# State-space stage of a two-block sequence model: decays from broadcast running sums, floor and exponential on ScalarE, mask on the scores, skip term in PSUM

## What is computed

```python
dt = softplus(dt_raw + dt_bias); a = -exp(a_log)
a_cs = cumsum(dt * a)                        # in each chunk of 128 tokens, one sum for each of 16 heads
cb = einsum("bclgn,bcsgn->bcgls", cc, bc)    # 2 groups of heads, state size 128
y_diag = einsum("bcgls,bcghls,bcsghp->bclghp", cb, exp_segsum(a_cs), xdt)   # exp(a_cs[l] - a_cs[s]) for s <= l, else 0
states = einsum("bclgn,bcghl,bclghp->bcghpn", bc, exp(a_cs[-1] - a_cs), xdt)
carry = carry * exp(a_cs[-1]) + states       # from chunk to chunk
y_off = einsum("bclgn,bcghpn,bcghl->bclghp", cc, prev, exp(a_cs))
y = y_diag + y_off + xs * d_skip
g = y * silu(z); ssm = g * rsqrt(mean(g * g) over a group + 1e-5) * w
```

## Time and profile before

| | before |
|---|---|
| median of three runs | 3471.3 us |
| profiled execution | 3469.94 us |
| its span | 3468.1 us |
| TensorE busy | 3187.7 us (92%) |
| VectorE busy | 1530.2 us (44%) |
| ScalarE busy | 1038.9 us (30%) |
| GpSimd busy | 1080.5 us (31%) |
| mean granted TensorE clock | 0.959 |

### The profile page before, as it was taken

The page is one execution under the profiler, slowest core; times in us unless marked ns, Lnnn a source line. Parts: engine busy times, 40 slices in busy tenths (PEclk is TensorE's granted clock), DMA queues, the critical chain, the costliest instruction groups (busy, mean ns, idle before and its releaser), DMA issues. The chain is left out here.

```text
span 3468.1 us, 49486 instructions
## 1 busy us (share of the span) xinstructions
PE 3187.7 (92%) x21000; PEld 2545.8 (73%) x21016; DVE 1530.2 (44%) x2122; ACT 1038.9 (30%) x1822; POOL 1080.5 (31%) x698
## 2 busy tenths in 40 slices
PE   5998799777999998989999998879899999988798
PEld 3885489665888877878777776658787777766587
DVE  3999645424222224341244343871312443438713
ACT  3012333313222222222244343530122444435401
POOL 2443022103333324323333332333233333323342
PEclk8999899898999999999999999989999999999899
DMA  5113200222111111222121224004221212240142
GB/s 198 49 49 118 102 4 4 77 87 74 48 48 48 48 30 61 97 79 75 49 79 49 67 92 154 11 34 143 84 76 48 80 49 68 91 157 8 36 144 76
DMA packets 210596, 250.71 MB, mean 72 GB/s; under 512 B 9280, under 2 KB 164032, under 8 KB 207968
## 3 DMA queue, kind: packets, MB, share of 16 engines
q1 hardware_dynamic: 199584, 208.02, 18.5%
q10 hardware_dynamic: 10240, 37.75, 2.8%
q0 software_dynamic: 576, 2.10, 0.2%
HBM read 199.60 MB, written 46.14 MB: 71 GB/s over the span
## 5 line engine op out<-in xcount | busy, mean ns | idle before, releaser
L1875 PE MATMUL PS<-x_high_sb,w_high_sb 128*128 128x512 f32 x1312 | 530.1, 404 | 0.0
L1875 PE MATMUL PS<-x_high_sb,w_low_sb 128*128 128x512 f32 x1312 | 518.2, 395 | 0.0
L1875 PE MATMUL PS<-x_low_sb,w_high_sb 128*128 128x512 f32 x1312 | 517.4, 394 | 0.0
L1875 PEld LDWEIGHTS PS<-x_high_sb,w_high_sb 128*128 128x128 f32 x1312 | 247.0, 188 | 76.1 <-issue 23.9
L1875 PEld LDWEIGHTS PS<-x_high_sb,w_low_sb 128*128 128x128 f32 x1312 | 246.9, 188 | 57.8
L360 PE MATMUL PS<-h_high_sb,up_high_sb 128*128 128x512 f32 x704 | 275.0, 391 | 13.5 <-POOL up_low_sb L1445 13.5
L1875 PEld LDWEIGHTS PS<-x_low_sb,w_high_sb 128*128 128x128 f32 x1312 | 247.3, 189 | 52.3
L360 PE MATMUL PS<-h_low_sb,up_high_sb 128*128 128x512 f32 x704 | 274.6, 390 | 0.0
L360 PE MATMUL PS<-h_high_sb,up_low_sb 128*128 128x512 f32 x704 | 274.6, 390 | 0.0
L1495 DVE SCALAR_TENSOR_TENSOR z_sb<-PS,cols_sb,z_sb 128x1023 f32<-128x1023 f32 x88 | 112.8, 1282 | 348.9 <-ACT z_sb L1476 342.5
L2112 DVE CUSTOM_DVE_ANT_0 scores_sb<-PS,alibi_sb,sinks_sb 128x256 f32<-128x256 f32 (+1 forms) x256 | 104.4, 464 | 341.8 <-PE PS L1893 341.6
(11 more groups left out here) (409 smaller groups left out, 6461.8 us busy)
## 6 DMA issues: line engine op xcount, KB each, us to landing
w_raw_sb<-w_in SPq DMA_DIRECT2D x102, 512.0 KB, 3.9
up_raw_sb<-w_up SPq DMA_DIRECT2D x44, 512.0 KB, 3.9
ada_slots_sb<-ada_w SPq DMA_DIRECT2D x16, 1024.0 KB, 5.5
w_raw_sb<-w_out SPq DMA_DIRECT2D x64, 256.0 KB, 2.8
xbc<-staged_sb ACTq DMA_DIRECT2D x24, 512.0 KB, 2.6
down_raw_sb<-w_down SPq DMA_DIRECT2D x44, 256.0 KB, 2.6
xbc_sb<-xbc SPq DMA_DIRECT2D x2, 5376.0 KB, 19.1
attn<-HT_sb ACTq DMA_DIRECT2D x8, 1024.0 KB, 4.9
```

The source lines that it names most:

```text
L1875: last = pe.matmul(PS[:, bank, :], a[:, n % 2, k], b[:, k, cols], start=k == 0 and a is WH and b is HH, stop=k == KT - 1 and a is WL)
```

## The change

`StepSizes` gains one TensorE transpose of the negated running sums, one ScalarE copy and one DMA that writes them to DRAM as 128 rows (chunk and head) of 128 tokens. In `state_space` the R products, the bf16 constants and the copy of X are gone. For each chunk one DMA loads the 16 rows of negated sums, each broadcast to all 128 partitions (1 MB), into one of three slots of E. ScalarE adds the positive sums as bias and floors the difference at zero (16 Relu instructions), and one Exp with scale -1 covers all 16 heads. The triangle mask is applied to the scores on VectorE (`masked`). The decays are multiplied in two instructions of eight heads (`weigh`). VectorE makes both products of x straight from PSUM (`inputs`), with dt folded into the decay to the end once. The skip term is a product with a diagonal matrix that TensorE adds up in the same PSUM banks as YD (`within`). The state has two buffers, and its scaling moves to GpSimd. The sums of squares are taken as 32-column products with 64 tokens each, so that root and reciprocal work on 64 columns, and four small products spread the result (`spread`). The order of each engine's program is new.

```diff
+        act.wait_ge(s.turned, 1)
+        nc.scalar.copy(self.tmp[:, 0], self.m.PS[:, 3, 0:TT * SH]).then_inc(s.ex, 1)
+        act.wait_ge(s.ex, 4)
+        act.dma_start(self.rows_d, self.tmp[:, 0]).then_inc(s.row_out, 16)
...
+        pe.transpose(self.m.PS[:, 3, 0:TT * SH], self.NA[:], self.m.const("ident")).then_inc(self.s.turned, 1)
...
-                    pe.wait_ge(step.s.ex, 3)
+                    pe.wait_ge(step.s.ex, 4)
...
+            act.wait_ge(step.s.row_out, 16)
...
+def state_space(m, d_skip, xbc_d, gate_d, rows_d, DT, A, NA, EI, DE, CD):
+    SLOTS = 3
-        RS = alloc(m, ctx, "inverse_rms", [P, 2, SG, P])
+        RS = alloc(m, ctx, "inverse_rms", [P, 2, HD])
-        E = alloc(m, ctx, "decays", [P, SH, P])
-        XS = alloc(m, ctx, "x_by_token", [P, DI])
-        XDT = alloc(m, ctx, "x_dt", [P, DI])
-        XDE = alloc(m, ctx, "x_dt_decayed", [P, DI])
+        E = alloc(m, ctx, "decays", [P, SLOTS, SH, P])
+        XDT = alloc(m, ctx, "x_dt", [P, 2, DI])
+        XDE = alloc(m, ctx, "x_dt_decayed", [P, 2, DI])
-        tmp = alloc(m, ctx, "y_tmp", [P, DI])
-        BC = alloc(m, ctx, "b_and_cb", [P, 512])
-        S = alloc(m, ctx, "state", [P, DI])
-        DS = alloc(m, ctx, "skip_rows", [P, SH])
+        BC = alloc(m, ctx, "b_and_cb", [P, 2, 512])
+        S = alloc(m, ctx, "state", [P, 2, DI])
+        SKIP = alloc(m, ctx, "skip_diagonal", [P, KT, P])
...
+            def rows(c):
+                sp.dma_start(E[:, c % SLOTS], rows_d[c * SH:(c + 1) * SH].unsqueeze(0).to_broadcast([P, SH, P])
+                             ).then_inc(row_in[c % SLOTS], 16)
+            rows(0)
+            sp.dma_start(XB[:, :, 0:P], xbc_d[:, :, 0:P].rearrange("k p t -> p k t")).then_inc(s.x_in0, 16)
+            sp.dma_start(skip[:], d_skip.to_broadcast([P, SH])).then_inc(s.skip_in, 16)
+            rows(1)
+            sp.dma_start(XB[:, :, P:T], xbc_d[:, :, P:T].rearrange("k p t -> p k t")).then_inc(s.x_in1, 16)
+            rows(2)
             sp.dma_start(ZS[:], gate_d.rearrange("k p t -> p k t")).then_inc(s.z_in, 16)
+            for c in range(SLOTS, TT):
+                sp.wait_ge(s.yd, c - SLOTS + 1)
+                rows(c)
...
+            def b_and_cb(c):
+                    pe.wait_ge(s.moved, c)
+                    pe.wait_ge(s.cb, c)
+                for g in range(SG):
+                    pe.transpose(PS[:, 4, g * P:(g + 1) * P], XB[:, KT + g, cols(c)], m.const("ident"))
+                for g in range(SG):
+                    last = pe.matmul(PS[:, 4, (2 + g) * P:(3 + g) * P], XB[:, KT + g, cols(c)],
+                                     XB[:, KT + SG + g, cols(c)], start=True, stop=True)
+                last.then_inc(s.b, 1)
+            def x_turned(c):
+                if c:
+                    pe.wait_ge(s.st_out, c)
...
+                last.then_inc(s.x, 1)
+            def from_state(c):
+                pe.wait_ge(s.st_out, c)
+                pe.wait_ge(s.y, c)
...
+                last.then_inc(s.yo, 1)
+            def to_state(c):
+                pe.wait_ge(s.moved, c + 1)
+                pe.wait_ge(s.xde, c + 1)
...
+                last.then_inc(s.st, 1)
+            def within(c):
+                pe.wait_ge(s.xdt, c + 1)
+                if c:
+                    pe.wait_ge(s.yo_out, c)
+                else:
+                    pe.wait_ge(s.small, 2)
+                for q in range(KT):
+                    pe.matmul(PS[:, 2 + q // 4, (q % 4) * P:(q % 4 + 1) * P], XB[:, q, cols(c)], SKIP[:, q],
+                              start=q % 4 == 0, stop=False, skip_group_check=True)
+                for h in range(SH):
+                    if h % 8 == 0:
+                        pe.wait_ge(s.masked, 2 * c + h // 8 + 1)
+                    last = pe.matmul(PS[:, 2 + h // 8, (h % 8) * HD:(h % 8 + 1) * HD], E[:, c % SLOTS, h],
+                                     XDT[:, c % 2, h * HD:(h + 1) * HD], start=False, stop=True, skip_group_check=True)
+                last.then_inc(s.yd, 1)
+            def y_turned(c):
+                pe.wait_ge(s.y, c + 1)
+                if c:
+                    pe.wait_ge(s.normed, c)
+                for q in range(KT):
+                    last = pe.transpose(PS[:, 6 + q // 4, (q % 4) * P:(q % 4 + 1) * P],
+                                        Y[:, c % 2, q * P:(q + 1) * P], m.const("ident"))
+                last.then_inc(s.g, 1)
+            def square_sums(c):
+                pe.wait_ge(s.squared, c + 1)
+                if c:
+                    pe.wait_ge(s.rooted, c)
+                for q in range(KT // SG):
+                    for r in range(4):
+                        g, a = r // 2, r % 2
+                        last = pe.matmul(PS[32 * r:32 * r + 32, 5, 0:HD], m.const("ones")[:, 0:32],
+                                         SQ[:, g * (KT // SG) + q, a * HD:(a + 1) * HD], start=q == 0,
+                                         stop=q == KT // SG - 1)
+                last.then_inc(s.ss, 1)
+            def spread(c):
+                pe.wait_ge(s.inverse, c + 1)
+                for a in range(2):
+                    for g in range(SG):
+                        r = slice(32 * (2 * g + a), 32 * (2 * g + a) + 32)
+                        last = pe.matmul(PS[:, 6 + g, a * HD:(a + 1) * HD], m.const("headpick")[r, 0:P], RS[r, c % 2],
+                                         start=True, stop=True)
+                    last.then_inc(s.spread, 1)
+                    if a == 0:
+                        pe.wait_ge(s.spread, 2 * c + 1)
...
+            b_and_cb(0)
+            x_turned(0)
+            for c in range(TT):
+                if c >= 2:
+                    spread(c - 2)
+                if c:
+                    from_state(c)
+                if c < TT - 1:
+                    to_state(c)
+                if c:
+                    y_turned(c - 1)
+                within(c)
+                if c + 1 < TT:
+                    if c == 0:
+                        pe.wait_ge(s.x_in1, 16)
+                    b_and_cb(c + 1)
+                    x_turned(c + 1)
+                if c:
+                    square_sums(c - 1)
+            spread(TT - 2)
+            y_turned(TT - 1)
+            square_sums(TT - 1)
+            spread(TT - 1)
...
+            def move(c):
+                act.wait_ge(s.b, c + 1)
+                if c >= 2:
+                    act.wait_ge(s.st, c - 1)
+                nc.scalar.copy(BC[:, c % 2, 0:2 * P], PS[:, 4, 0:2 * P]).then_inc(s.moved, 1)
+            def exps(c):
+                e = E[:, c % SLOTS]
+                act.wait_ge(row_in[c % SLOTS], 16 * (c // SLOTS + 1))
+                for h in range(SH):
+                    at = c * SH + h
+                    nc.scalar.activation(e[:, h], e[:, h], ACT.Relu, bias=A[:, at:at + 1]).then_inc(s.floored, 1)
+                act.wait_ge(s.floored, SH * (c + 1))
+                nc.scalar.activation(e, e, ACT.Exp, scale=-1.0).then_inc(s.exps, 1)
...
+            def root(c):
+                act.wait_ge(s.ss, c + 1)
+                if c >= 2:
+                    act.wait_ge(s.spread, 2 * c - 2)
+                nc.scalar.activation(RS[:, c % 2], PS[:, 5, 0:HD], ACT.Sqrt, scale=1.0 / GW, bias=eps).then_inc(s.rooted, 1)
+            act.wait_ge(s.kept, 1)
+            move(0)
+            exps(0)
+            for c in range(TT):
+                if c:
+                    square(c - 1)
+                if c + 1 < TT:
+                    move(c + 1)
+                    exps(c + 1)
+                if c:
+                    root(c - 1)
+            square(TT - 1)
+            root(TT - 1)
...
+            for c in range(1, TT - 1):
+                pool.wait_ge(s.st_out, c)
                 if c >= 2:
+                    pool.wait_ge(s.yo, c - 1)
+                nc.gpsimd.tensor_tensor(by_head(S[:, (c + 1) % 2]), by_head(S[:, c % 2]), wide(CD, c), ALU.mult
+                                        ).then_inc(s.grown, 1)
...
+            def masked(c):
+                dve.wait_ge(s.moved, c + 1)
+                if c >= 2:
+                    dve.wait_ge(s.masked, 2 * c - 2)
+                v.tensor_tensor(BC[:, c % 2, 2 * P:4 * P].rearrange("p (g n) -> p g n", g=SG),
+                                PS[:, 4, 2 * P:4 * P].rearrange("p (g n) -> p g n", g=SG),
+                                m.const("tri").unsqueeze(1).to_broadcast([P, SG, P]), ALU.mult).then_inc(s.cb, 1)
+            def weigh(c):
+                dve.wait_ge(s.exps, c + 1)
+                dve.wait_ge(s.cb, c + 1)
+                for g in range(SG):
+                    e = E[:, c % SLOTS, 8 * g:8 * g + 8]
+                    cb = BC[:, c % 2, (2 + g) * P:(3 + g) * P].unsqueeze(1).to_broadcast([P, SH // SG, P])
+                    v.tensor_tensor(e, e, cb, ALU.mult).then_inc(s.masked, 1)
+            def inputs(c):
+                dve.wait_ge(s.x, c + 1)
+                if c >= 2:
+                    dve.wait_ge(s.yd, c - 1)
```

(56 more changed lines are left out.)

191 lines of the change are left out of this document (29 added, 162 removed).

## The result

The changed kernel takes 3538.93 us (median of 4 runs, 3537.68 to 3539.89), the kernel before 3471.32 on the same chip (3470.49 to 3471.89). The ratio is 1.0195, 95% interval 1.0177 to 1.0212: slower, by 67.6 us. The forecast was 3535 us, range 3497 to 3567.

The account below looks back on a forecast made before the run. It took a ring through GpSimd and ST (20.5 us a chunk) as the old bound, a serial ring of 25.4 as the new. At +32 us a layer, 3469.94 + 64 = 3534, said as 3535 us; range 3497 to 3567.

Parts of the forecast that it names:

- The chain: Twelve steps in series from the end of one YD to the next: 23.4 us, 25.4 with the clock.
- 16 Relu: ScalarE's Relu instructions of 128 columns in each chunk: 0.27 us apiece, 4.4 us together, bounds 2.2 and 6.2.
- `weigh`: VectorE's two multiplications of the decays, priced as undisturbed by GpSimd: 2.4 us against 6.8 for the four before.
- clock, in all: TensorE idles some 7 us a chunk, so `spread` and `from_state` run at 1.2 GHz: 2.0 us more a chunk.
- the ring: In-order programs tie one `within` to the next through ScalarE's exponentials, `weigh`, reciprocal, `spread` and `from_state`: 25.4 us a chunk.
- rival C: ScalarE's exponentials of the next chunk run beside `within`, so TensorE sets the pace, some 17 us a chunk: 3428 us, chance 0.06.
- signs named beforehand: YD additions 25 us apart, ScalarE in one 8 us block, `weigh` 1.2 us an instruction, granted clock near 0.85.
- Sums of squares: TensorE's products beneath ScalarE's exponential work in each chunk: 2 us.
- Chunk 1: First step of the stage, without `spread` and with `from_state` early: 17.8 us, with the clock 20, against 18.95 before.
- start: Up to the end of YD(0): 0 give or take 1.5 us; with the projection stage's 0.5, +0.5 a layer.
- end: After the last YD, sums of squares through normalise for the last chunks: 14.7 to 16.5 us against 14.05, +1.5.
- The ring through GpSimd and ST: Kernel before: copy of X, three GpSimd products, ST, SS, YD, B, R0, next X set each chunk's 20.5 us.

Follow-up runs that it names:

- run 2: Changed kernel with nine unread fp32 products on TensorE behind the sums of squares of chunks 0 to 5, keeping it busy over the gap: 3516.91 us.
- run 1: Changed kernel with TensorE issuing spread(c-2) behind from_state(c) and to_state(c) instead of ahead of them: 3504.83 us, ratio 1.0091 to the kernel before.
- run 3: Changed kernel with one Relu over all 16 heads, using the first head's running sum, in place of 16: 3498.3 us.
- run 5: Changed kernel with the same computing instructions reordered on TensorE, VectorE and ScalarE, and rows of chunks 1 and 2 loaded behind XB: 3406.48 us, ratio 0.981.
- Run 7: Changed kernel with only the loads moved, the broadcast rows of chunks 1 and 2 behind the rest of XB: 3536.64 us.
- run 6: Kernel before the change, with GpSimd's decayed product moved ahead of its skip product: 3495.03 us, ratio 1.0059.
- run 8: Kernel of run 5 with the exponentials begun before the copy of B and the mask moved right before the weighing: 3416.36 us, ratio 0.9838.
- run 9: Kernel of run 8 with chunk 1 of xbc and chunk 0 of the gate loaded first as small transfers: 3405.56 us, ratio 0.981.
- run 10: Kernel of run 9 with weighing ahead of the gate, B's copy between Relu and exponential, and GpSimd's state scaling awaiting one more gate: 3366.55 us, ratio 0.9698.

## Why the prediction was right, and where not

**The chain.** Right, nearly step by step. Forecast and measured in the middle chunk shown above (us):

| step | forecast | measured |
|---|---|---|
| B and its copy | 1.0 | 0.94 |
| 16 Relu | 4.4 | 4.78 |
| table load, exponential | 1.38 + 1.9 | 1.30 + 1.94 |
| `weigh` | 2.4 | 2.27 |
| reciprocal, handover | 0.6 | 0.60 |
| `spread` | 1.0 | 1.4 (slow clock in it) |
| `from_state` | 1.9 | 3.8 (slow clock in it) |
| scaling and normalise | 2.4 | 2.5 |
| `y_turned`, skip, YD | 1.0, 1.8, 3.7 | 0.9, 1.8, 3.7 |
| clock, in all | 2.0 | in the two rows above, 2.3 by run 2 |
| a chunk | 25.4 | 25.95 |

That the ring closes through ScalarE's block, the reciprocal and `spread` is shown by three runs from three sides: `spread` moved behind `from_state` (run 1), ScalarE's block cut (run 3), the whole ring opened (run 5). The point at which rival C would have decided, whether the first Relu precedes the last YD record, is what the rows show against it: the copy of B has 3.66 us idle before it, ended by TensorE's L2239, and the first Relu starts at 2237.80, behind the last record of YD. Of the signs named beforehand one did not come: the granted clock over the seven steps is 0.77 and 0.76, not near 0.85.

**The terms that were mis-sized.** The 16 Relu take 0.30 us apiece, not 0.27: +0.4 a chunk. Sums of squares were reckoned at 2 us and took 0.65 for 32 records (2238.29). They lay beneath ScalarE's block, so this took nothing off the step; it is 1.35 us of what made the gap ahead of `spread` 9.76 us where I had said some 7. The 0.4 of the Relu and 0.3 of the clock, less small terms of the other sign, are the 0.5 us that were missing in the chunk shown. It is one of the longest: chunks 2 to 6 of layer 1 take 25.6 us in the mean.

**Chunk 1.** Forecast 20 us, measured 22.45 and 21.47. The step that failed is the one that let XB's rest arrive "about to when it is needed". TensorE's record of B in chunk 1:
```profile
2166.83 0.69 PE L2237 MATMUL PS<-consts_sb,xbc_sb 128*128 128x128 f32 x2 [3.04 <-DMA xbc_sb<-xbc]
```
3.04 us idle, ended by the load. From YD(0) to the first Relu it is 4.84 us (2163.84 to 2168.68) where I had 1.0, and 3.86 in layer 2. A second term was wrong the other way: I had charged chunk 1 a table load, and there is none, since no root runs between the two exponentials; the last Relu ends at 2173.46 and the exponential starts at 2173.49. The clock is the third: ahead of the skip products TensorE is idle for 3.76 us, and they and YD(1) take 7.2 us in place of 5.5. Run 7 takes the rows from ahead of XB and the step of layer 1 falls to 19.64, under the forecast 20. In layer 2 it does not fall, because the clock takes more there than the load gives back. So the load's order explains what the forecast missed in chunk 1, and the clock decides what mending it is worth.

**Chunk 7.** No `to_state` stands between `from_state` and `y_turned` there, so TensorE has a second idle of 2.54 us and the clock stays down longer: `y_turned` 1.94, skip 2.59, in place of 1.06 and 1.95.
```profile
2333.89 1.94 PE L2288 MATMUL PS<-consts_sb,y_sb 128*128 128x128 f32 x8 [2.54 <-DVE HT_sb L2435]
```
The last step is 27.4 where I took 25.4. Before, the last step was like the others. I had multiplied one chunk by six and had not walked the last.

**Start, end and sum.** Per layer, forecast in brackets: start -1.6 with the projection stage in it (+0.5), steps +35.8 (+30.2), end 13.55 against 14.05, so -0.5 (+1.5). Of the 5.6 us that the steps are longer, chunk 1 has 2.4, chunk 7 has 2.0 and the five between them 1.1. The start is shorter because TensorE began only 2.0 us later (2148.70 against 2146.74), where I had 3 to 4.7. The end was added up wrongly: the terms in the prediction come to 14.0 us, and the 14.7 to 16.5 beside them has no term for the rest; measured were 13.55, with the sums of squares at 0.65 and 1.08 us instead of 2 and more. Together the three give +33.7 in layer 1, +67.3 for two layers by layer 1's numbers; measured +67.6. Forecast +64. The errors a layer, +5.6 in the steps and -4.1 in start and end, have nothing to do with each other. That they cancelled for the most part, and the total is better than its terms, is luck.

**The kernel before.** The ring through GpSimd and ST was one of two of the same length, as run 6 shows. The forecast did not rest on it: it took the 20.5 us from the trace, and the change takes away both. But the reading would have misled anyone who wanted to mend that kernel, as it misled run 6.

**GpSimd and VectorE.** `weigh` was priced as undisturbed, and is: 2.36 us for two. GpSimd's one product left takes 1.90 us in the changed kernel; before, a product of that shape took 2.34 beside VectorE's multiplication of the decays. This agrees with the other half of the Trainium skill's rule (SBUF — State Buffer, section Who interferes with whom), that one SBUF input does not contend: beside GpSimd's product (2257.56 to 2259.46) VectorE ran the gate, with one input from SBUF, in 1.23 us, its usual length.

**What stays open.** Whether TensorE's clock falls at a gap of about 1 us: run 5 has both under one program (YD takes 4.85 us behind a gap of 0.92 us at 2232.31, and 3.79 us behind one of 0.92 at 2201.10 and one of 1.00 in layer 2), run 2 has both after 1.84 us. Runs 8 to 10 show only the two ends: with 1.45 us ahead of the product within the chunk (runs 8 and 9) most steps were slow, and with 0.32 us (run 10) none was.

## What to carry to other kernels

When a rewrite takes work from the busiest engines, draw the ring before adding the sums: start at the product that ends a round, and follow each in-order program to the next one, naming what stands in front of every wait. The cure for such a ring is order before less work. One Relu in place of 16 gave 40.6 us (run 3), the other order 132 us (run 5): in layer 1 the seven steps took 177.9 us in the order of the change and 118.9 with the same instructions in another (run 5), and 92.4 once no short gap was left ahead of the longest product and the first loads were cut small (run 10). After a mend, look at what now stands right ahead of TensorE's longest product, since a gap there can be paid twice, once as idle time and once in the clock behind it.
